# Sixteen expert products of a diffusion step: from three reduced-precision passes of split operands to native fp32 products on 64- and 32-column strips

## What is computed

```python
def ec_moe(h, router_w, w_gate, w_up, w_down):
    B, T, D = h.shape
    cap = EC_CAPACITY * T // N_EXPERTS
    aff = jax.nn.softmax(jnp.einsum('btd,de->bte', h, router_w, preferred_element_type=jnp.float32), axis=-1)
    gate, idx = lax.top_k(jnp.swapaxes(aff, 1, 2), cap)
    flat = idx.reshape(B, N_EXPERTS * cap)
    xg = jnp.take_along_axis(h, flat[..., None], axis=1).reshape(B, N_EXPERTS, cap, D)
    a = jax.nn.silu(jnp.einsum('becd,edf->becf', xg, w_gate)) * jnp.einsum('becd,edf->becf', xg, w_up)
    y = jnp.einsum('becf,efd->becd', a, w_down) * gate[..., None].astype(h.dtype)
    return jnp.zeros_like(h).at[jnp.arange(B)[:, None], flat].add(y.reshape(B, N_EXPERTS * cap, D))
```

## Time and profile before

| | us |
|---|---|
| median of 3 runs | 1311.96 (1307.42 to 1312.77) |
| the profiled execution | 1309.95 |
| its span, first to last instruction | 1308.2 |
| TensorE busy | 1203.7 (92%) |
| VectorE busy | 990.9 (76%) |
| ScalarE busy | 727.6 (56%) |
| mean granted TensorE clock | 0.960 |

### The profile page before, as it was taken

How to read it: one execution, slowest core, us unless ns; L and a number is a source line. 1 busy time by engine, 2 the same in 40 slices (tenths; PEclk the granted TensorE clock), 3 DMA queues, 4 the chain that set the end, 5 groups by cost and what they waited for, 6 DMA issues and landing times.

```text
span 1308.2 us, 18212 instructions
## 1 busy us (share of the span) xinstructions
PE 1203.7 (92%) x6845; PEld 919.5 (70%) x6845; DVE 990.9 (76%) x976; ACT 727.6 (56%) x770; POOL 341.4 (26%) x192
## 2 busy tenths in 40 slices
PE   5889999999998978779898799999999999999995
PEld 3567888888987967669777366666666666666663
DVE  2787335565178787878855789999999999999993
ACT  3313325555467758462412477777777777777772
POOL 1022000121000010100001002555666655555422
PEclk7889999999998989789999699999999999999998
DMA  8620521211331222144634699999999999999992
GB/s 310 236 80 24 202 97 38 73 42 59 96 117 54 70 90 78 72 154 162 227 129 156 235 399 393 393 392 386 391 382 385 389 387 391 380 394 387 390 365 49
DMA packets 111858, 296.06 MB, mean 226 GB/s; under 512 B 7092, under 2 KB 33076, under 8 KB 111800
## 3 DMA queue, kind: packets, MB, share of 16 engines
q1 hardware_dynamic: 108280, 284.25, 58.1%
q0 software_dynamic: 3520, 11.01, 3.7%
HBM read 278.47 MB, written 16.78 MB: 226 GB/s over the span
## 4 chain that ended last, share of the span: by engine, by line
PE 49%; DVE 3%; ACT 1%; issue 0%; DMA 0%; POOL 0%; DVEq 0%; ACTq 0%; POOLq 0%
PE ps L1759 15%; PE ps L1760 15%; PE ps L1761 15%; PE ps L2084 1%; PE ps L2100 1%; DVE arena L1343 1%; PE ps L2059 1%; DVE w_lo L1219 0%; PE ps L2046 0%; PE ps L1789 0%; DMA arena<-xn_rows,arena 0%; ACT w_hi L942 0%; DVE arena L1598 0%; DVE arena L1594 0%; PE ps L1857 0%
## 5 line engine op out<-in xcount | busy, mean ns | idle before, releaser
L1759 PE MATMUL ps<-w_hi,act_hi 128*80 128x512 f32 (+1 forms) x856 | 342.6, 400 | 13.6 <-DVE w_lo L1219 4.9
L1678 DVE TENSOR_TENSOR w_lo<-arena,w_hi 128x2048 fp32r<-128x2048 f32 x144 | 325.5, 2286 | 23.7 <-ACT w_hi L1173 17.5
L1760 PE MATMUL ps<-w_lo,act_hi 128*80 128x512 f32 (+1 forms) x856 | 338.0, 395 | 0.0
L1761 PE MATMUL ps<-w_hi,act_lo 128*80 128x512 f32 (+1 forms) x856 | 336.9, 394 | 0.0
L1173 ACT ACTIVATE w_hi<-arena 128x2048 fp32r<-128x2048 f32 x135 | 258.6, 1918 | 93.9 <-PE ps L1761 93.9
L1759 PEld LDWEIGHTS ps<-w_hi,act_hi 128*80 128x80 f32 (+1 forms) x856 | 139.5, 163 | 78.9 <-issue 6.6
L1759 PE MATMUL ps<-act_hi,w_hi 128*128 128x320 f32 x576 | 184.3, 320 | 5.8 <-DVE w_lo L1219 2.8
L1761 PEld LDWEIGHTS ps<-w_hi,act_lo 128*80 128x80 f32 (+1 forms) x856 | 139.3, 163 | 59.6 <-issue 0.9
L1760 PE MATMUL ps<-act_lo,w_hi 128*128 128x320 f32 x576 | 179.0, 311 | 0.0
L1761 PE MATMUL ps<-act_hi,w_lo 128*128 128x320 f32 x576 | 178.9, 311 | 0.0
L1760 PEld LDWEIGHTS ps<-w_lo,act_hi 128*80 128x80 f32 (+1 forms) x856 | 139.7, 163 | 55.4 <-issue 0.9
(11 more groups left out here) (229 smaller groups left out, 1700.6 us busy)
## 6 DMA issues: line engine op xcount, KB each, us to landing
arena<-in_w_exp_gate_dram SPq DMA_DIRECT2D x64, 1024.0 KB, 8.5
arena<-in_w_exp_up_dram SPq DMA_DIRECT2D x64, 1024.0 KB, 7.6
arena<-in_w_exp_down_dram SPq DMA_DIRECT2D x64, 1024.0 KB, 7.5
arena<-in_w_mod_dram SPq DMA_DIRECT2D x23, 1024.0 KB, 5.2
arena<-in_w_in_dram SPq DMA_DIRECT2D x18, 1024.0 KB, 7.0
arena<-in_w_in_dram SPq DMA_DIRECT2D x12, 512.0 KB, 5.5
gl_raw<-arena SPq DMA_DIRECT2D x32, 160.0 KB, 1.8
arena<-gl_raw SPq DMA_DIRECT2D x8, 640.0 KB, 10.1
```

The lines of the kernel that those rows point to most:

```text
L1678: v.tensor_tensor(EWl[sl], eraw[slot], EWh[sl].bitcast(F32), ALU.subtract).then_inc(s_el, 1)
L1759: t.matmul(out, sh, mh, start=start, stop=False)
L1760: t.matmul(out, sh, ml, start=False, stop=False)
L1761: return t.matmul(out, sl, mh, start=False, stop=stop)
```

## The change

- The split and everything that serves it goes: the float32r copies, their semaphores, the ScalarE and VectorE instructions. Weights are read by TensorE straight from the buffers that the DMAs fill.
- A piece is made of native fp32 products. The 64 latent tokens are stationary on two strips of 64 columns, one for each half of the 1024 output columns (bank 2 pr). The context tokens, padded from 16 to 32 with zeros, stand on four strips of 32 columns, one for each quarter (bank 2 pr + 1). Silu and the product with up are then 128 x 768 in place of 80 x 1024.
- Hidden values are turned by six transposes of 128 x 128, and copied once (`hT`). The product of down is first gathered into rows by six ScalarE copies (`ycopy` into `yr`), from which VectorE scales it.
- Nine raw buffers in place of six, freed by `s_eu` (a piece multiplied) in place of `s_el` (a piece split). SP issues nine pieces before the stage, without a wait for the first gather; the last modulation piece goes ahead of the fifth of them.
- The loops over experts are written out on each engine. The step "top" stands ahead of the last modulation product. The turned tokens have two buffers.

```diff
-        NRE = 6
-        eraw = [part(0, 2048), part(2048, 2048), part(4096, 2048)] + raw
+        NRE, NP = 9, 12 * NE
+        eraw = [arena[:, o_vso:o_vso + 2048], part(0, 2048), part(2048, 2048), part(4096, 2048), part(8192, 2048), part(10240, 2048)]
+        XW, HW = CAP_LAT + 32, 512 + 256
...
-        STEPS += [("rt", 2), ("rt", 3), ("hT", 4), ("aff", 0), ("h2e", 4), ("rt", 4), ("aff", 1), ("mod", 10), ("g2", 10), ("eh",),
-                  ("mod", 11), ("top",)]
+        STEPS += [("rt", 2), ("rt", 3), ("hT", 4), ("aff", 0), ("h2e", 4), ("rt", 4), ("aff", 1), ("mod", 10), ("g2", 10),
+                  ("top",), ("mod", 11)]
...
+            epiece(0)
             sp.wait_ge(s_yrow, 16 * NT)
-            sp.wait_ge(s_xn2, NT)
+            for n in range(1, 4):
+                epiece(n)
+            load(len(PIECES) - 1)
             sp.wait_ge(s_sq2, NT)
...
+            filled(sp, ("logits", 1))
+            epiece(4)
+            filled(sp, ("affT", 1))
+            epiece(5)
+            for n, key in enumerate((("mod", 10, 1), ("mod", 11, 0), ("mod", 11, 1))):
+                sp.wait_ge(*used[key])
+                epiece(6 + n)
+            for n in range(NRE, NP):
+                sp.wait_ge(s_eu, n - NRE + 1)
+                epiece(n)
...
+            def ycopy(e):
+                act.wait_ge(s_eu, down_made(e))
+                if e:
+                    act.wait_ge(s_y, e)
+                y = pair(2 if e + 1 < NE else 0)
+                for b in range(2):
+                    a.activation(yr[0:CAP_LAT, 512 * b:512 * b + 512], y[64 * b:64 * b + 64, 0:512], ACT.Copy)
+                for s in range(4):
+                    ins = a.activation(yr[CAP_LAT:CAP, 256 * s:256 * s + 256], y[32 * s:32 * s + CAP_CTX, 512:HW], ACT.Copy)
+                ins.then_inc(s_yr, 1)
+
+            for e in range(NE):
+                act.wait_ge(s_eu, gate_made(e))
+                if e:
+                    act.wait_ge(s_aT, e)
+                a.activation(aa[:, 0:HW], pair(0)[:, 0:HW], ACT.Silu).then_inc(s_silu, 1)
+                if e:
+                    ycopy(e - 1)
                 act.wait_ge(s_aT, e + 1)
...
+                a.activation(hT, pair(3)[:, 0:HW], ACT.Copy).then_inc(s_ahi, 1)
+            ycopy(NE - 1)
...
-            def piece_mm(pr, ready, sl, hi_, lo_, j):
-                pe.wait_ge(s_el, ready)
-                wh, wl = (w[sl].rearrange("p (k n) -> p k n", k=2) for w in (EWh, EWl))
+            def piece_mm(n, pr, of, src, j):
+                pe.wait_ge(s_er[n % NRE], 16 * (n // NRE + 1))
+                w = eraw[n % NRE].rearrange("p (k n) -> p k n", k=2)
                 for kk in range(2):
                     kt = 2 * j + kk
+                    lat, ctx_ = of(src, kt)
                     for b in range(2):
-                        cs = slice(512 * b, 512 * b + 512)
-                        ins = mm3(bank(2 * pr + b)[0:CAP, :], (hi_[:, kt, :], lo_[:, kt, :]), (wh[:, kk, cs], wl[:, kk, cs]), kt == 0, kt == 7)
+                        t.matmul(bank(2 * pr)[64 * b:64 * b + 64, :], lat, w[:, kk, 512 * b:512 * b + 512], start=kt == 0, stop=kt == 7)
+                for kk in range(2):
+                    kt = 2 * j + kk
+                    lat, ctx_ = of(src, kt)
+                    for s in range(4):
+                        ins = t.matmul(bank(2 * pr + 1)[32 * s:32 * s + 32, 0:256], ctx_,
+                                       w[:, kk, 256 * s:256 * s + 256], start=kt == 0, stop=kt == 7)
                 ins.then_inc(s_eu, 1)
```

More of the change, by code:

```diff
@@ L916, in _ @@
             pool.wait_ge(s_gt, 5)
-            with pool.Fori(2, NE - 1) as e:
+            for e in range(2, NE - 1):
                 gather(e + 1)
@@ L1160, in body @@
-            def body(e, last=False):
-                for j in range(12):
-                    ehi_at(e, j)
-                    if j == 3:
-                        ahi(e - 1)
-                    if j == 7:
-                        silu(e)
-                    if j == 11 and not last:
-                        xhi(e + 1)
-            def ehi_at(e, j):
-                act.wait_ge(s_er[(j + 2) % NRE], (e * 2 + (j - 4) // 6 + 1) * 16)
-                act.wait_ge(s_eu, e * 12 + (j - 7))
-                a.activation(EWh[j % NEW], eraw[(j + 2) % NRE], ACT.Copy).then_inc(s_eh, 1)
@@ L1696, in alo, with hidden @@
-            def alo(e):
-                dve.wait_ge(s_ahi, e + 1)
-                v.tensor_tensor(al, xpsum, ah.bitcast(F32), ALU.subtract).then_inc(s_alo, 1)
-            def yout(e, pr=2, first=False):
-                dve.wait_ge(s_eu, min(e * 12 + 20, 12 * NE) if isinstance(e, int) else e * 12 + 20)
-                if not first:
+                v.tensor_tensor(xT[e % 2][:, :, 0:CAP], xT[e % 2][:, :, 0:CAP], B2f, ALU.add).then_inc(s_xgf, 1)
+            def hidden(e):
+                dve.wait_ge(s_silu, e + 1)
+                dve.wait_ge(s_eu, up_made(e))
+                v.tensor_tensor(aa[:, 0:HW], aa[:, 0:HW], pair(1)[:, 0:HW], ALU.mult).then_inc(s_a, 1)
@@ L1703, in yout @@
+            def yout(e):
+                dve.wait_ge(s_yr, e + 1)
+                if e:
                     dve.wait_ge(s_scat, 32 * e)
-                v.scalar_tensor_tensor(out=ye[0:CAP, :], in0=pair(pr)[0:CAP, :], scalar=gT[0:CAP, bass.ds(e, 1)], in1=G2[0:CAP, :],
+                v.scalar_tensor_tensor(out=ye[0:CAP, :], in0=yr[0:CAP, :], scalar=gT[0:CAP, e:e + 1], in1=G2[0:CAP, :],
                                        op0=ALU.mult, op1=ALU.mult).then_inc(s_y, 1)
-            def body(e, first=False, second=False, last=False):
-                for j in range(12):
-                    elo(j % NEW, e * 12 + (j - 3), (j + 2) % NRE)
-                    if j == 1 and first:
-                        hidden(0, 8)
-                    if j == 3:
-                        alo(e - 1)
-                    if j == 4 and not first:
-                        yout(e - 2, first=second)
-                    if j == 9 and not last:
-                        xmod(e + 1)
-                    if j == 10:
-                        hidden(e, e * 12 + 4)
-                    if j == 11 and not last:
-                        xlo(e + 1)
@@ L1740, in _ @@
-            xlo(1, (xh1, xl1))
-            body(1, first=True)
-            body(2, second=True)
-            with dve.Fori(3, NE - 1) as e:
-                body(e)
-            body(NE - 1, last=True)
-            for n in range(188, 191):
-                elo(n % NEW, n + 1, n % NRE)
-            alo(NE - 1)
-            yout(NE - 2)
-            elo(191 % NEW, 192, 191 % NRE)
-            yout(NE - 1, 0)
+                v.tensor_tensor(x0, x0, B2f[:, k4, :], ALU.add).then_inc(made, 1)
+            for e in range(NE):
+                if e + 1 < NE:
+                    xmod(e + 1)
+                hidden(e)
+                if e:
+                    yout(e - 1)
```

215 lines of the change are left out of this document (75 added, 140 removed).

## The result

The kernel after takes 1342.32 us, the median of 4 runs (1341.05 to 1343.96); the kernel before, 1310.26 over its 4 runs (1307.42 to 1312.77). The ratio is 1.0246, with a 95% interval of 1.0219 to 1.0274: **slower by 2.5%**. The prediction said 1341.

What follows compares the result with a forecast made beforehand. TensorE was taken to bound the expert stage; pieces 19.6, turns 4.4, start 2, end 0.7 and 2.4 sum to +29.1 us on the 1311.96 median, 1341 us. The main case's own ends were 1328 to 1354, with 0.8 in 1311 to 1357.

Steps and rivals of the forecast that it cites:

- What bounds: Expert stage: TensorE sets the pace with no waits of its own, one expert taking 34.16 us and a piece 2.753.
- A piece: Expert stage: 64-wide block 1.855 us plus 32-wide block 1.00, two width changes included; 0.102 more per piece, +19.6 us over 192.
- rival 2: Strip-width changes within expert pieces: only one direction costs, -28 us against the main case, 1313, no change; chance 0.09.
- Rival 1: Strip-width changes in the expert stage are free: a piece is 2.58 us, total about 1290; chance 0.06.
- Turns: Transposes in the expert stage: turn of tokens 0.65 us, of hidden values 0.75, +4.4 us in all.
- The cover: Expert stage: removed splits are worth nothing; DMA at 373 GB/s stays ahead with nine buffers and costs nothing.
- The start: Before the first expert piece: lists some 1.4 us sooner, first gather slower under load, bounds -1.4 and +2.9; +2 us.
- loaded median: First gather at the stage's start: gathers land 8.5 us after issue at the median under load, 4.2 at best.
- The end: Last expert: copies of expert 14's product make PE idle 2.5 us, +0.7; six copies after the last product, +2.4.
- Rival 3: Expert stage: stream not fed or strips disturb each other beside full DMA, 5% on a piece, +27 us, 1368; chance 0.09.

## Why the prediction was right

The forecast was +29.1 us on the median of that time, 1341; the kernel after stands at 1342.32, inside the range. The mechanism came out as forecast, and the largest term, the piece, to an eighth of its own size; the terms at the start and the end were off by 1 to 4 us each, in both directions. Term by term:

- **What bounds.** TensorE sets the pace before and after, without a wait in the stage. VectorE's busy time fell by 455 us and ScalarE's by 331, and that bought nothing, as forecast.
- **A piece.** Forecast 1.855 + 1.00, measured 1.868 + 1.00: a piece 0.013 us above the forecast, 2.5 us over 192. The split that the prediction guessed, a width change of 0.1 and the rest in the first group behind it, is what the records show: 100 ns on leaving the 64-wide strips and 51 on entering them, 113 and 24 for the 32-wide. The step from 64 to 32, which no row showed, costs like the others; rival 2 falls by 529 against 429 ns.
- **The width change itself** was an inference from rows of other stages. It is now shown by altering it alone: half of the changes, twice, and none, gave 1320, 1397 and 1297 around the 1342. The double blocks, half blocks and equal-width blocks fit one set of numbers to 0.01 us, 429 and 216 ns a group, 100 or 113 a change, 51 or 24 behind it. Rival 1, a free width change, falls by the same runs. The time that it would have given was about 1290, the lead of nine buffers covering DMA for the most part. The kernel without width changes took 1296.69, with the weights' stream as the next bound from the twelfth turn on.
- **Turns.** Forecast 0.65 and 0.75, measured 0.70 and 0.80; +1.6 us over 31 turns.
- **The stage in sum.** First piece to last turn grew by 26.2 us. The forecast of this part was 19.6 + 4.4 less the last turn, some 23.4, and with 2.4 and 1.5 of it for the pieces and turns in this part it would be 27.3. Against that stand 1.3 us of the first pieces, which ran at the lower clock until 750.5 before, and until 748.6 now: 26.0.
- **The cover.** DMA was to fall to 373 GB/s and did, 373 in the stretch shown. The prediction expected its share to fall as well; it went from 1.03 to 1.02. Nine buffers cost and gained nothing.
- **The start.** Forecast: lists 1.4 us sooner, gather loaded, +2 in all. The lists' idle went from 1.82 to 0.41 and the gather took 8.7 us in place of 4.3, at its loaded median and not between the bounds where the prediction put it. From the first row of the lists to the first piece it is 14.2 us, before 9.7: +4.5, less the 1.4, +3.1 for the edit. The span shows +0.7, as everything ahead of the lists ended 2.4 us sooner in this execution.
- **The end.** The idle of 2.5 us was 2.90 and the copies' 2.4 were 2.8. **Missing from the sum was what the idle does to the clock**: it fell behind the 2.90 us, so that the first two blocks took 5.48 us (1312.71 to 1318.19) in place of 2.87, and the third 2.07 in place of 1.87: 2.8 us. The prediction said of the stage that it would be wrong if the clock fell there. It fell, at the one place where PE stood idle; the price was under a tenth of the change's. The part is +7.2; the forecast had 3.7 for it (0.7 and 2.4, and 0.2 for the turn and 0.4 for four pieces that lie in it).
- **Rival 3**, strips that disturb each other beside full DMA. There is none of it: equal-width blocks of four strips run at 429 ns per 512 columns with 392 GB/s beside them. The Trainium skill, "TensorE: Matmul & The Clock Gate", section "Measured speedup vs the span model", has three 32-wide tiles at 2.38 times; here four native fp32 strips give their full four times: four records of 512 columns in 429 ns, 0.84 ns a column, where a record of the full-width transposes, alone in the array, takes 109 ns for 128 columns, 0.85. The measurement decides.

In sum the medians differ by 32.1 us where 29.1 were forecast. The spans of the two profiled executions differ by 34.0, 4.9 above the forecast: pieces and turns 4 us and the end 3.5 above it, the start 1.3 under it, the first pieces' clock 1.3 under it again. That the total came so near is in part luck, as these misses cancel in part, and the 2.4 us by which everything ahead of the lists ended sooner in this execution were no term of the forecast.

Left open: why the clock fell behind 2.9 us of idle in the kernel after, in its repeat (for 6.8 us each) and in the four variants that keep 64-wide blocks and that order of copies (6.8 or 3.4 us), and did not behind the same 2.9 us in the two without width changes that have it. And what a stream of weights above 390 GB/s would need; no run here tried other transfer sizes.

## What to carry to other kernels

When products of different widths share the array in column strips, count the changes of width, in the order in which TensorE meets them, as a cost of their own: here 0.14 to 0.15 us each with the slower first group behind it, two for every 2.6 us of streaming, turned a gain of 1% into a loss of 2.5%. Where one width divides the other, write the wide product as two narrow ones; here the outputs landed in the same places, the extra loads were hidden, and the stream ran at its full rate. Where such an edit makes TensorE faster, ask at once whether the weights come as fast: here a period 1.6 us under what the stream fed (32.74 against 34.36, the mean of the last four distances) was paid for by a lead of nine buffers for the first 350 us of the stage, and the rest waited.

## What the runs showed of the hardware

- A change of strip width costs 100 ns on TensorE at 2.4 GHz from 64 to 32 and 113 from 32 to 64, and the first group behind it 51 (64-wide) or 24 ns (32-wide) more. From 32-wide work to the full-width transposes it is 114 ns. Going from the 32-wide blocks of one kind to another (512 to 256 columns) costs nothing.
- Two native fp32 products of 64 stationary columns side by side and four of 32 take the same 429 ns for 512 moving columns, with twice the weight loads in the second.
- Around 2.9 us of idle TensorE's clock went to its lower level, for 6.8 us in three profiles and 3.4 in three more of the eight that have that idle; around 0.90 us, in four profiles, it never fell.
- The first indirect gather of 80 rows was used 4.3 us after its issue with the loads ahead of it landed, 6.1 in the run with six buffers, 8.7 with nine.
- The DMA engines' busy share was 1.02 at 373 GB/s and 1.03 at 380 to 384 with time to spare, and 1.03 at 390 when TensorE waited for them. What told them apart, at nine buffers each, was the time from issue to landing: 8, 11 and 17 us. With six buffers and TensorE waiting it was 13.
